# Narrow row tiles of two input projections on column groups of the array

## The reference

```
def _mixer_ab(xn, ...):
    u = xn @ w['ab_w_in'][j]
    qkv, beta_in, a_in, z_dn, gq, gk, gv, g_lr, z_gla = _split(u, AB_SIZES)
    ...
    beta = jax.nn.sigmoid(beta_in)
    g = -jnp.exp(w['dn_a_log'][j]) * jax.nn.softplus(a_in + w['dn_dt_bias'][j])
    ...
    glog = jax.nn.log_sigmoid(g_lr @ w['gla_wa2'][j] + w['gla_ba'][j]) / GLA_GATE_NORM
def _mixer_cd(xn, ...):
    u = xn @ w['cd_w_in'][j]
    z, xbc, dt_in, z_lru, x_lru = _split(u, CD_SIZES)
    ...
    dt = jax.nn.softplus(dt_in + w['ssd_dt_bias'][j])
```

## Time and profile before

| | us |
|---|---|
| median of 3 runs (2452.65 to 2455.01) | 2453.15 |
| the profiled execution | 2456.65 |
| its span, first to last instruction | 2454.7 |
| PE busy (97%) | 2385.0 |
| DVE busy (52%) | 1284.3 |
| ACT busy (39%) | 958.4 |
| POOL busy (15%) | 371.3 |

### The profile page before, as it was taken

One profiled execution on the slowest core, in us unless ns is written; L12 is line 12 of the kernel. 1 busy time (PEld: TensorE's weight loads), 2 busy tenths in 40 slices (PEclk: granted clock), 3 DMA queues, 4 the chain that ended last, 5 costly groups with the idle time before them and its releaser, 6 DMA issues.

```text
span 2454.7 us, 50321 instructions
## 1 busy us (share of the span) xinstructions
PE 2385.0 (97%) x21567; PEld 2275.4 (93%) x21567; DVE 1284.3 (52%) x2387; ACT 958.4 (39%) x1547; POOL 371.3 (15%) x558
## 2 busy tenths in 40 slices
PE   7999999999999999999999999999999999999996
PEld 6999999988899999899999999988899989999996
DVE  6655655565654564722354465566656653243432
ACT  5523444333444344432342253433355553243332
POOL 3101111111101101111111212122212211111110
PEclk9999999999999999999999999999999999999998
DMA  9333333333343454552234343233323354233232
GB/s 249 87 107 107 116 102 112 91 112 102 107 119 110 142 149 122 182 178 88 82 94 115 103 120 91 67 92 85 87 80 102 95 193 123 87 86 92 78 89 75
DMA packets 375534, 271.15 MB, mean 110 GB/s; under 512 B 24419, under 2 KB 346733, under 8 KB 374800
## 3 DMA queue, kind: packets, MB, share of 16 engines
q1 hardware_dynamic: 341424, 172.53, 26.0%
q0 software_dynamic: 22080, 72.77, 9.2%
q10 hardware_dynamic: 11808, 22.63, 2.6%
HBM read 220.24 MB, written 48.37 MB: 109 GB/s over the span
## 4 chain that ended last, share of the span: by engine, by line
PE 55%; DVE 2%; ACT 1%; DMA 1%; issue 0%; ACTq 0%; POOL 0%; DVEq 0%; POOLq 0%
PE psd L582 48%; PE psw L605 2%; PE psw L604 1%; PE psw L660 0%; PE psw L971 0%; PE psw L682 0%; PE psw L963 0%; PE psw L951 0%; DVE w_lo L1684 0%; DMA arena<-hT_scratch 0%; PE psw L668 0%; PE psw L674 0%; ACT arena L1250 0%; DVE xl L1744 0%; DVE arena L1824 0%
## 5 line engine op out<-in xcount | busy, mean ns | idle before, releaser
L582 PE MATMUL psd<-xh,w_hi 128*128 128x272 f32 x5056 | 1100.4, 299 | 14.9 <-DVE w_lo L1684 6.1
L582 PE MATMUL psd<-xh,w_lo 128*128 128x272 f32 x5056 | 1048.6, 289 | 0.0
L582 PE MATMUL psd<-xl,w_hi 128*128 128x272 f32 x5056 | 1046.3, 288 | 0.0
L582 PEld LDWEIGHTS psd<-xh,w_hi 128*128 128x128 f32 x5056 | 796.7, 189 | 66.3 <-issue 38.1
L582 PEld LDWEIGHTS psd<-xl,w_hi 128*128 128x128 f32 x5056 | 797.8, 189 | 0.0
L582 PEld LDWEIGHTS psd<-xh,w_lo 128*128 128x128 f32 x5056 | 793.2, 190 | 0.0
L1684 DVE TENSOR_TENSOR w_lo<-w_raw,w_hi 128x512 fp32r<-128x512 f32 x632 | 437.2, 711 | 379.5 <-ACT w_hi L1136 378.4
L1136 ACT CAST w_hi<-w_raw 128x512 fp32r<-128x512 f32 x632 | 376.6, 615 | 577.5 <-PE psd L582 499.6
L2580 POOL TENSOR_TENSOR states<-states,extra 128x544 f32<-128x544 f32 x59 | 86.8, 1471 | 513.9 <-ACT extra L1191 513.8
L2376 DVE TENSOR_TENSOR extra<-psd,rstd 128x544 f32<-128x544 f32 x32 | 23.2, 724 | 157.5 <-PE psd L582 140.4
L2349 DVE TENSOR_TENSOR arena<-arena,psd 128x544 f32<-128x544 f32 x32 | 23.0, 719 | 136.5 <-PE psd L582 130.2
(11 more groups left out here) (514 smaller groups left out, 2371.3 us busy)
## 6 DMA issues: line engine op xcount, KB each, us to landing
w_raw<-in_ab_w_in_dram SPq DMA_DIRECT2D x224, 256.0 KB, 3.0
w_raw<-in_cd_w_in_dram SPq DMA_DIRECT2D x148, 256.0 KB, 3.0
w_raw<-in_ple_w_gate_dram SPq DMA_DIRECT2D x128, 256.0 KB, 3.1
w_raw<-in_ab_w_out_dram SPq DMA_DIRECT2D x64, 256.0 KB, 2.9
w_raw<-in_cd_w_out_dram SPq DMA_DIRECT2D x64, 256.0 KB, 2.9
uT_scratch<-mix ACTq DMA_DIRECT2D x53, 272.0 KB, 2.4
hT_scratch<-arena POOLq DMA_DIRECT2D x8, 1088.0 KB, 6.3
arena<-hT_scratch POOLq DMA_DIRECT2D x8, 1088.0 KB, 9.8
```

The lines of the kernel that those rows point to most:

```text
L582: mm = pe.matmul(out[:, D0 + HALF * half:D0 + HALF * (half + 1)], w[:, r, k % QH, :], x[:, k, HALF * half:HALF * (half + 1)], start=(k == ...
```

## The change

- Each rows tile has 32 weight columns in use. In "ab" they are 16 columns from beta and 16 from g_lr; SP loads two runs of 64 columns (256 bytes) per row. In "cd" they are the 32 columns from dt on.
- ACT copies them, unsplit, to `w_full` (which lies where `w_hi` lies). DVE's subtraction goes over 32 columns per slice and its result is not used.
- `rows_slice` takes the place of the six matmuls: four fp32 products, one per slice of the quarter, each into its own 32 PSUM partitions, for one half of the tokens and one of `xh`, `xl`. Four such calls cover a quarter.
- Four partial sums then lie on four groups of partitions. DVE evicts them to `rowG`, a new group "rq" multiplies by the 0/1 matrix `gather` (made by POOL), which adds them and puts the rows where they were, and ACT copies the result to `rowlr`.
- In "cd" the rows tile is the second tile now.
- DVE makes the masks and selectors behind `rows_ab` instead of ahead of it.

```diff
-    tiles.insert(1, ("ab", 0, (AB_BETA, AB_A, AB_LR, AB_LR), "ab", None, "rows"))
+    tiles.insert(1, ("ab", 0, (AB_BETA, AB_LR), "ab", None, "rows"))
...
-    tiles += [("cd", 0, (CD_DT,), "cd", None, "rows")]
-    tiles += [("cd", 0, (CD_XBC + SSD_W + P * c,), "cd", ("bc", 0), "x") for c in range(4)]
+    bc = [("cd", 0, (CD_XBC + SSD_W + P * c,), "cd", ("bc", 0), "x") for c in range(4)]
+    tiles += bc[:1] + [("cd", 0, (CD_DT,), "cd", None, "rows")] + bc[1:]
...
+FILL = {("ab_rows", "rq"): 0.15, ("cd_rows", "rq"): 0.5, ...
...
-                width = P // len(starts)
+                width = 64 if len(starts) == 2 else used_columns(q)
...
+            def rows_slice(out, k, r):
+
+                quarter, s = k // QH, k % QH
+                x, half = (xh, xl)[s // 2], slice(HALF * (s % 2), HALF * (s % 2 + 1))
+                for j in range(QH):
+                    mm = pe.matmul(out[32 * j:32 * j + 32, D0 + half.start:D0 + half.stop], w_full[:, r, j, 0:ROW_COLS],
+                                   x[:, QH * quarter + j, half].bitcast(F32),
+                                   start=(quarter == 0 and s < 2), stop=(quarter == NQ - 1 and s >= 2))
+                mm.then_inc(S["slice_done"], 1)
...
+                if TILES[d][5] == "rows":
+                    rows_slice(out, k, r)
+                    return
...
+            def gathered_rows(u, d):
+
+                W = group(u, "rq")
+                pe.wait_ge(S["pool_chain"], 2)
+                pe.wait_ge(S[f"dense_read{d % 2}"], d // 2 + 1)
+                all_tokens(W, gather[:, :], rowG[:, :], start=True, stop=True).then_inc(S["work_ready"], 1)
...
+                    n = len(TILES[q // NQ][2])
+                    act.copy(w_full[:, q % NW, :, 0:ROW_COLS].rearrange("p k (s c) -> p k s c", s=n),
+                             w_raw[:, q % NW].rearrange("p k (s c) -> p k s c", s=n)[:, :, :, 0:ROW_COLS // n])\
...
+            def gathered_rows(u, n):
+
+                W = group(u, "rq")
+                act.copy(rowlr[:, :], W[:, WT]).then_inc(S["rows_copied"], 1)
+                act.wait_ge(S["rows_copied"], n)
...
-                act.wait_ge(S[f"dense_read{d % 2}"], d // 2 + 1)
+                gathered_rows(("ab_rows", 0), 1)
...
-            dve.wait_ge(S["params_loaded"], PARAM_DMAS * 16)
-            go(dve.tensor_copy(masks[:, 0:CUT].rearrange("p (i j) -> p i j", i=2), negm.unsqueeze(1).broadcast_to([P, 2, P])))
...
                 if u[0] == "ab_rows":
                     rows_ab()
                     skip(u, "c0")
+                    constants()
```

More of the change, by code:

```diff
@@ L32 @@
 D0 = SEQ - HALF
+ROW_COLS = 32
 CUT = SEQ // 2
@@ L138, in group_table @@
         if kind == "ab_rows":
+            once(unit, "rq", "rows_copied")
             once(unit, "c0", "rows_copied")
@@ L232, in trunk @@
         w_raw = sb("w_raw", [P, NW, QH, P])
+        with nc.sbuf_tensor("w_full", [P, NW, QH, P], F32) as w_full:
+            pass
         w_hi, w_lo = sb("w_hi", [P, NW, QH, P], F32R), sb("w_lo", [P, NW, QH, P], F32R)
@@ L257, in trunk @@
         rowR, onehot = sb("rowR", [P, T], F32R), sb("onehot", [P, 2, SSD_H], F32R)
+        gather = sb("gather", [P, P])
         rstd = sb("rstd", [P, T])
@@ L514, in y_tokens, with used_columns @@
             return arena[:, :].rearrange("p (c t) -> p c t", c=KT)[:, :, P * t:P * t + P]
+        def used_columns(q):
+            return ROW_COLS if TILES[q // NQ][5] == "rows" else P
         block = ctx.enter_context(nc.Block())
@@ L1085, in _ @@
                 if u[0] == "ab_rows":
+                    gathered_rows(u, ROWS["ab"])
                     columns_of_rows(u)
@@ L1100, in _ @@
                 if u[0] == "cd_rows":
+                    gathered_rows(u, ROWS["cd"])
                     W = group(u, "eg")
@@ L1135, in split_hi @@
                     act.wait_ge(S["slice_done"], quarter_end(q - NW))
+                if TILES[q // NQ][5] == "rows":
+                    n = len(TILES[q // NQ][2])
+                    act.copy(w_full[:, q % NW, :, 0:ROW_COLS].rearrange("p k (s c) -> p k s c", s=n),
+                             w_raw[:, q % NW].rearrange("p k (s c) -> p k s c", s=n)[:, :, :, 0:ROW_COLS // n])\
+                       .then_inc(S["hi_ready"], 1)
+                    return
                 act.copy(w_hi[:, q % NW], w_raw[:, q % NW]).then_inc(S["hi_ready"], 1)
@@ L1683, in split_lo @@
                 dve.wait_ge(S["hi_ready"], q + 1)
-                dve.tensor_tensor(w_lo[:, q % NW], w_raw[:, q % NW], w_hi[:, q % NW].bitcast(F32),
+                n, r = used_columns(q), q % NW
+                hi = w_full if TILES[q // NQ][5] == "rows" else w_hi.bitcast(F32)
+                dve.tensor_tensor(w_lo[:, r, :, 0:n], w_raw[:, r, :, 0:n], hi[:, r, :, 0:n],
                                   ALU.subtract).then_inc(S["lo_ready"], 1)
@@ L2397, in gate, with constants @@
                     lo_part(3, KT - 1)
+            def constants():
+                dve.wait_ge(S["params_loaded"], PARAM_DMAS * 16)
+                go(dve.tensor_copy(masks[:, 0:CUT].rearrange("p (i j) -> p i j", i=2), negm.unsqueeze(1).broadcast_to([P, 2, P])))
+                go(dve.tensor_copy(masks[:, CUT:CUT + NS], negs))
+                for j in range(4):
+                    r = slice(32 * j, 32 * j + 32)
+                    go(dve.tensor_copy(C32[r, 0, :], MT[r, 0, 32 * j:32 * j + 32]))
+                    go(dve.tensor_copy(C32[r, 1, :], ib16[r, 32 * j:32 * j + 32]))
+                    go(dve.tensor_copy(C32[r, 2:6, :], MX[r, 1:5, 32 * j:32 * j + 32]))
+                    go(dve.tensor_copy(mine2[r], rowm[:, 2 * j:2 * j + 2]))
+                    if j < 2:
+                        go(dve.tensor_copy(mine4[r], rowm[:, 4 * j:4 * j + 4]))
+                wait_chain()
+                for m in range(2):
+                    go(dve.tensor_tensor(sel[:, m], bc4(C32[:, 1, :]), mine2[:, m:m + 1].unsqueeze(2).broadcast_to([P, 4, 32]),
+                                         ALU.mult))
+                wait_chain()
             dve.memset(ones[:, :], 1.0)
@@ L2541, in _ @@
             pool.memset(small[:, :], 0.0)
+            pool.memset(gather[:, :], 0.0)
             link(pool.memset(hist[:, :, :], 0.0))
@@ L2572, in _ @@
             pool.dma_start(wa2[64:64 + GLA_R, :], I["gla_wa2"][0]).then_inc(S["rows_loaded"], 16)
+            pool.wait_ge(S["consts_loaded"], 16)
+            for j in range(4):
+                r = slice(32 * j, 32 * j + 32)
+                for to, at, n in ((0, 0, 16), (32, 8, 8), (64, 16, 16)):
+                    ins = pool.tensor_copy(gather[r, to:to + n], ident[r, 32 * j + at:32 * j + at + n])
+            link(ins)
             def add_square(i, c):
```

25 lines of the change are left out of this document (6 added, 19 removed).

## The result

| | before | after |
|---|---|---|
| median of 8 runs each | 2453.6 us (2452.17 to 2457.08) | 2459.86 us (2456.49 to 2466.44) |
| the same kernel again, with 11 runs (before: 32) | 2454.0 us (2449.2 to 2460.62) | 2456.84 us (2454.02 to 2460.77) |
| profiled execution, its span | 2456.65, 2454.7 | 2459.86, 2458.1 |

The ratio is 1.0025 (95% interval 1.0016 to 1.0035) in the first comparison and 1.0011 (1.0003 to 1.0020) in the second: the change makes the kernel 3 to 6 us slower. I had predicted 2450.0 us with a range up to 2454.5; it is outside, on the other side of the kernel before.

A forecast was written before the change was run, and what follows sets the result against it. TensorE, busy 97% of the span, was taken as the bound. Second layer 3.5 us plus first layer 0.1 less 0.5 gave 3.1 us off the 2453.15 us median: 2450.0 us, range 2442.5 to 2454.5.

The forecast's parts named there:

- The narrow products: Both rows tiles: four column groups run together, 0.47 us a slice, 7.5 us a tile of 16 slices.
- the rival of groups in series: Rows tiles: the four groups run one behind the other, 29.8 us a tile, total 2487 us; chance 0.06.
- The second layer: Its rows tile shrinks from 12.02 to 7.5 us, less 0.93 for the gather and 0.1: 3.5 us gained.
- The landing of the last block: First layer's rows tile: its last block lands at 51.0 us instead of 52.5.
- The clock: First layer behind the block wait: quarter 3 at 0.50 (3.7 us), three slices half at each level (3.2 us).
- The chain behind the gather: First layer, ACT and DVE: the first head's squares are done 39.5 us after the gather's end.
- the break-even of 63.7 us: First layer: the gather's end at which it neither gains nor loses; 63.6 us was forecast.
- PE's new wait: First layer, first head's sums of squares: PE waits 3.3 us there, whenever the gather ends.
- The first layer turned out dearer: Rival: gather's end at 65.3 us, another 0.50 stretch (1.7 us) at the squares, total 2453 us; chance 0.14.
- The early landing: Rival: last rows block lands at 46 us, gather's end 56.7, total gain 10 us, 2443 us; chance 0.36.
- The forecast of 0.1 us for it, less 0.5: First layer's sum: 0.1 us gained against break-even, 0.5 taken off for ACT work standing 2 us later behind PE.

The follow-up runs named there:

- cd_only: Kernel before with only the second projection's rows tile narrow (with its gather, as the second tile); median 2450.49 us.
- loads_late: Changed kernel, but POOL issues the constants and the two ssd_d broadcast loads only when ACT has copied the last rows block; median 2450.37 us.
- cb_late: Changed kernel, but POOL issues the load of the constants (722 KB) only when ACT has copied the last rows block; median 2455.76 us.
- ab_only: Kernel before with only the first projection's rows tile narrow (with its gather and the constants behind it); median 2461.49 us.
- none_late: Kernel before with constants and broadcasts loaded behind the last rows block, constants computed behind the rows work, no narrow rows tile; median 2449.71 us.
- egt_early: Changed kernel with the two broadcast loads of ssd_d issued by POOL ahead of the store of h; median 2455.17 us.
- pe_filled2: Changed kernel with 14 extra fp32 products in PE's wait before the first rows tile's last quarter, into the next group's free buffer; median 2452.24 us.
- both_late2: loads_late run a second time, unchanged; median 2447.44 us.
- ab_late: none_late with the first projection's rows tile narrow; median 2451.00 us.
- cd_late2: Second run of loads_late with the first projection's rows tile as in the kernel before, only the second's narrow; median 2445.91 us.

## Why the prediction was wrong

**The narrow products: right.** 0.46 us a slice in both layers, 0.47 forecast; the rival of groups in series falls. The Trainium skill (TensorE: Matmul & The Clock Gate, "The mechanism") states that weight loads overlap running products only where the row group differs. The trace does not agree: with all four column groups in one row group and weight loads of 121 ns, a slice of 0.46 us is 0.23 per pass, which is what 272 columns cost at the earlier trace rows with no weight load in between.

**The second layer: right.** 3.5 us forecast, 3.43 in every trace, -3.5 in the work of cd_only; no new wait at line 1103's product. The gather's group there takes part in this sum with 0.93 us, of which 0.70 us lie between its first product and the next slice (64.09 and 64.79 at the start) and the rest in that slice.

**The landing of the last block: wrong, and the first step that failed.** I took 51.0 us, "0.8 from the first three blocks no longer running into the store of h, 0.7 from the shorter remainder". It was 53.3 to 53.9, later than before. With half as many packets the block gained nothing, because what it waited for was neither the number of its packets nor the bulk of the other queue alone. I had read from the strip that most engines were idle and had said that it "waits for the engines that come last out of their software packets"; that was right, but I priced it as if those engines then still had to move a part of the block in proportion to its packets. What held them were packets of two broadcasts, 4 KB in all, which I had not looked at: in before their last one ends at 51.2 us, and loads_late, which differs from cb_late in them alone, has the block 9.0 us earlier.

In the Trainium skill (DMA: Bandwidth & Descriptors, "Queues, rings and completion order") each DMA engine takes turns between the queues it has work for, packet by packet, and a packet is several descriptors. The counts of the earlier trace rows, 889 to 907, would fit turns of one profile packet each, but from 31 to 39.5 us they are 488 to 657 in after and 977 to 708 in loads_late, and no run shows what a turn is. What I missed needs no such rule: the time of the other queue's packets, not their number, was what the block waited for.

**The clock: right in kind, too small.** It is the second step that failed. I took 3.7 us for the last quarter at the lower clock, and half of the three slices behind the transposes. In the first trace the gather's end was at 64.79 us, in the second at 68.06, where the clock stayed at 0.50 for 17 us; 63.6 was forecast. I had transferred the stretch of before, behind a wait of 3.9 us, to a wait twice as long. On average over the executions, ab_only spends 7.3 us more at 0.50 than before.

**The chain behind the gather: right.** Squares done 39.5 us after the gather's end was the forecast; 103.71 + 1.11 = 104.82 is 40.0 us after 64.79. Measured from the break-even of 63.7 us, a gather's end at 64.79 costs 1.1 us and one at 68.06 costs 4.4; with the chain of 40.0 it is 0.5 more each. The shift against before behind the squares is 1.84 us in the first trace. In the second it is 6.65: 5.0 up to the product of the squares and the rest the clock that the new wait brought with it. PE's new wait there was 2.0 us where I said 3.3. PE itself came 1.9 us later than I had it, the squares 0.5: the transposes of the rows wait 1.2 us for DVE (line 732), which I had not foreseen. That wait moves with the chain and costs nothing of its own as long as PE waits for the squares. What ended PE's new wait were ACT's squares, and ACT had waited 12.8 us for DVE's convolution.

**The rivals.** The first layer turned out dearer, which I gave 0.14. Its condition was a gather's end at 65.3 us and another stretch at 0.50 at the new wait; the two traces have 64.79 without the stretch and 68.06 with it. But I priced the rival at 2453 from one execution and let no case stand beyond it, although the same rows put 1 us on the end for each us of a late landing. The early landing got 0.36 from packet counts, against a strip that spoke plainly. That an early landing helps is shown by loads_late, 3.8 us faster than before where the rival said 10.

**What the first layer could have given.** The forecast of 0.1 us for it, less 0.5, lies at the mild end of what it gives when the block lands in time: between 0 and 3 us lost, in the two pairs of kernels with late loads. What I had put on the early landing, 7 us for the first layer, comes from the landing and not from the narrow form: none_late has 5.5 us of it without the narrow form (by the medians, against before).

## What to carry to other kernels

Where an engine already waits for a transfer, less work on it is worth nothing and can cost: the wait grows by what is saved (3.90 to 7.59 us here), and in these traces TensorE's clock fell in the longer wait and stayed down behind it. Find first what the transfer waits for, by the time of each queue's packets and not their number: here two strided broadcasts of 2 KB in another queue held a block of 256 KB for 9.0 us. Then ask of each saving what chain hangs behind it: the same form that gave 3.4 us where products stood back to back gave nothing where a chain of other engines came next.

## What the runs showed of the hardware

- Packets of 128 bytes, which spread elements of 4 bytes, took 1.7 to 3.7 us each (31 of 32 in after; up to 4.1 in egt_early), against 0.018 us for the 256-byte runs of a weight block and 0.45 us for 5776-byte rows of the constants (records of after). In loads_late the two broadcasts of 2 KB took 12.8 us from issue to landing and the 722 KB ahead of them 7.5.
- Issued at 10.5 us, among the loads of x, they delayed the first dense slice by 5.7 us (egt_early).
- Four fp32 products in four column groups ran at 0.115 us each for 272 columns (0.46 a slice), although they share one row group and change weights on each product.
- The lower clock came within a wait of 7.6 to 8.2 us and stayed for 6.8 us and, after 3.4 at full clock, 3.4 more, or for 17 us; with products in that wait it did not come (pe_filled2). In loads_late and both_late2 it came without such a wait, behind small transposes (of 24 and 32 rows), for 3.4 and 6.8 us; in pe_filled2, ab_late and cd_late2 the same transposes did not bring it.
- Executions of one kernel differ by 3 to 13 us, with mean clocks of 0.986 to 0.993; the product of span and clock has a standard error of 0.2 to 1.1 us a kernel.
